# A two-block network in float32 on one core: start by feature tiles, GpSimd's products behind level 0, ScalarE's order in level 5

## What is computed

```python
def _mixer_gdn(h, w_in, conv_w, a_log, dt_bias, norm_g, w_out):
    proj = jnp.matmul(h, w_in)                      # 512x1024 @ 1024x4128
    qkv = silu(depthwise_conv(proj[..., :3072], conv_w))
    z, ba = proj[..., 3072:4096], proj[..., 4096:]  # ba: the gates
    ...                                             # q, k l2-normed per head
    beta = sigmoid(ba[:, :, 0])
    g = -exp(a_log) * softplus(ba[:, :, 1] + dt_bias)
    o = gated_delta(q, k, v, beta[0], g[0]) + flip(gated_delta(flip(q, k, v, beta[1], g[1])))
    o = rmsnorm(o, norm_g) * silu(z)                # per head
    return o @ w_out
```

## Time and profile before

| | |
|---|---|
| median of 3 runs | 2045.12 us |
| the profiled execution | 2043.4 us, span 2041.6 us |
| TensorE products | 1881.9 us busy (92%) |
| VectorE, ScalarE, GpSimd | 997.9, 726.0, 239.4 us busy |
| granted clock of TensorE, mean | 0.964 of 2.4 GHz |

### The profile page before, as it was taken

One profiled execution on the slowest core, in us unless ns is written; L12 is line 12 of the kernel. 1 busy time (PEld: TensorE's weight loads), 2 busy tenths in 40 slices (PEclk: granted clock), 3 DMA queues, 4 the chain that ended last, 5 costly groups with the idle time before them and its releaser, 6 DMA issues.

```text
span 2041.6 us, 24057 instructions
## 1 busy us (share of the span) xinstructions
PE 1881.9 (92%) x9070; PEld 1512.0 (74%) x9070; DVE 997.9 (49%) x1408; ACT 726.0 (36%) x1177; POOL 239.4 (12%) x226
## 2 busy tenths in 40 slices
PE   6999999999889999999799888889999998799989
PEld 6887778888668887887577677668887886575667
DVE  2775455555374444445321456464444366513653
ACT  2434544444222223322342343232223334434440
POOL 2001243343000001000000234000000000200410
PEclk8999999999989999999899999989999998899999
DMA  3223100000323324221222100423235231421001
GB/s 123 83 82 103 62 1 1 1 1 1 125 68 96 94 91 137 86 100 62 62 83 83 62 1 1 145 83 103 82 103 180 88 103 42 134 78 62 1 1 62
DMA packets 101442, 146.72 MB, mean 72 GB/s; under 512 B 4673, under 2 KB 70289, under 8 KB 101104
## 3 DMA queue, kind: packets, MB, share of 16 engines
q1 hardware_dynamic: 94272, 119.29, 18.6%
q0 software_dynamic: 6512, 24.20, 3.3%
q10 hardware_dynamic: 576, 2.10, 0.3%
HBM read 143.47 MB, written 2.10 MB: 71 GB/s over the span
## 4 chain that ended last, share of the span: by engine, by line
PE 86%; DVE 7%; ACT 3%; issue 2%; DMA 1%; POOL 1%; ACTq 0%; DVEq 0%; POOLq 0%; SPq 0%
PE bk L261 21%; PE bk L263 21%; PE bk L262 21%; PE bk L953 3%; PE bk L972 2%; PE bk L1711 1%; PE bk L2459 1%; PE bk L2460 1%; PE bk L963 1%; PE bk L2479 1%; ACT whi L246 1%; PE bk L940 1%; DVE wlo L252 1%; PE bk L1075 1%; PE bk L1014 1%
## 5 line engine op out<-in xcount | busy, mean ns | idle before, releaser
L252 DVE TENSOR_TENSOR wlo<-raw,whi 128x1024 fp32r<-128x1024 f32 x224 | 266.5, 1229 | 480.0 <-ACT whi L246 475.6
L261 PE MATMUL bk<-act_hi,whi 128*128 128x512 f32 (+1 forms) x1024 | 412.1, 402 | 7.6 <-DVE act_lo L387 5.0
L262 PE MATMUL bk<-act_lo,whi 128*128 128x512 f32 (+1 forms) x1024 | 409.2, 400 | 0.0
L263 PE MATMUL bk<-act_hi,wlo 128*128 128x512 f32 (+1 forms) x1024 | 409.0, 399 | 0.0
L246 ACT ACTIVATE whi<-raw 128x1024 fp32r<-128x1024 f32 x224 | 226.3, 1052 | 366.0 <-PE bk L263 327.7
L261 PE MATMUL bk<-whi,act_hi 128*128 128x512 f32 x768 | 310.7, 405 | 32.0 <-DVE act_lo L536 17.9
L263 PE MATMUL bk<-whi,act_lo 128*128 128x512 f32 x768 | 310.6, 404 | 0.0
L262 PE MATMUL bk<-wlo,act_hi 128*128 128x512 f32 x768 | 309.0, 402 | 0.0
L261 PEld LDWEIGHTS bk<-act_hi,whi 128*128 128x128 f32 (+1 forms) x1024 | 194.6, 190 | 60.2 <-issue 6.7
L262 PEld LDWEIGHTS bk<-act_lo,whi 128*128 128x128 f32 (+1 forms) x1024 | 194.7, 190 | 48.1 <-issue 0.7
L263 PEld LDWEIGHTS bk<-act_hi,wlo 128*128 128x128 f32 (+1 forms) x1024 | 194.5, 190 | 48.1
(11 more groups left out here) (372 smaller groups left out, 2381.0 us busy)
## 6 DMA issues: line engine op xcount, KB each, us to landing
raw<-in_mlp_w SPq DMA_DIRECT2D x128, 512.0 KB, 4.3
raw<-in_a_w_in SPq DMA_DIRECT2D x32, 512.0 KB, 4.5
work<-in_w_mod POOLq DMA_DIRECT2D x3, 4096.0 KB, 15.9
raw<-in_b_w_in SPq DMA_DIRECT2D x24, 512.0 KB, 3.9
raw<-in_w_in SPq DMA_DIRECT2D x14, 512.0 KB, 4.7
raw<-in_a_w_out SPq DMA_DIRECT2D x8, 512.0 KB, 4.0
raw<-in_b_w_out SPq DMA_DIRECT2D x8, 512.0 KB, 4.0
raw<-in_w_out SPq DMA_DIRECT2D x8, 512.0 KB, 3.9
```

Of the source, the lines that this page charges most:

```text
L252: nc.vector.tensor_tensor(wlo[b][:, hs], raw[hf][:, :], whi[b][:, hs], ALU.subtract).then_inc(w_ready, 1)
L261: nc.tensor.matmul(acc, lhs_hi, rhs_hi, start=first, stop=False, skip_group_check=True)
L262: nc.tensor.matmul(acc, lhs_hi, rhs_lo, start=False, stop=False, skip_group_check=True)
L263: return nc.tensor.matmul(acc, lhs_lo, rhs_hi, start=False, stop=last, skip_group_check=True)
```

## The change

- The identity is loaded first on SyncE's queue, then the left half of x's columns, half of slab 0, the right half, the other half of the slab. ScalarE's queue loads nothing any more. `tri`, `negpair`, parity and the gates' two vectors are issued by GpSimd at the end, after a wait for the right half of x. The convolution weights have a semaphore of their own.
- x is turned by feature tiles: one tile (4 transposes) fills one bank. The first output tile of slab 0 (bank 0) is multiplied feature tile by feature tile as these become ready, and tiles 4 to 7 are turned between the products. The second output tile (bank 1) follows, and then the gates. Slab 0 is split by halves among the split of the tiles on ScalarE and VectorE.
- GpSimd waits for `z` at 14h + 2 (level 0 done) before the logs and before the next head's decays; mask and start of Z stay ahead.
- ScalarE in level 5: the Ln of the head before comes ahead of the copies to X, in the place of the row exponential; the row exponential and then the Exp follow the copies.

```diff
+        def x_half(i):
+            return a["x"][0][:, i * 512:i * 512 + 512].rearrange("(t p) n -> p t n", p=P)
+
         def sp_start(sp):
-            for b in range(2):
-                load_slab(sp, 0, b, slab_source("a_in", 0, b))
-
-        def act_start(act):
-            for st in range(ST):
-                act.dma_start(X[:, st, :], a["x"][0, st * P:st * P + P, :]).then_inc(x_loaded, 16)
-
-        NCONST = 5
+            source = slab_source("a_in", 0, 0)
+            sp.dma_start(eye[:, :], a["k_eye"]).then_inc(eye_loaded, 16)
+            for i, loaded in enumerate((x_loaded, x_rest_loaded)):
+                sp.dma_start(X[:, :, i * 512:i * 512 + 512], x_half(i)).then_inc(loaded, 16)
+                sp.dma_start(slab_view(raw[i], KT // 2), source[:, i * KT // 2:(i + 1) * KT // 2, :]).then_inc(raw_loaded[i], 16)
+            load_slab(sp, 0, 1, slab_source("a_in", 0, 1))
+
+        NCONST = 4
         def pool_start(pool):
-            pool.dma_start(eye[:, :], a["k_eye"]).then_inc(eye_loaded, 16)
...
-            pool.dma_start(A["tri"], a["k_tri"].rearrange("p (m s) -> p m s", m=4)).then_inc(const_loaded, 16)
-            pool.dma_start(A["negpair"], a["k_negpair"].rearrange("p (m s) -> p m s", m=LEVELS)).then_inc(const_loaded, 16)
-            pool.dma_start(A["parity"], a["k_parity"]).then_inc(const_loaded, 16)
-            pool.dma_start(gwv["dt"], a["a_dt_bias"][0].rearrange("d h -> (d h)").partition_broadcast(P)
-                           ).then_inc(G["w_loaded"], 16)
-            pool.dma_start(gwv["alog"], a["a_alog"][0].rearrange("d h -> (d h)").partition_broadcast(P)
-                           ).then_inc(G["w_loaded"], 16)
...
+            pool.wait_ge(x_rest_loaded, 16)
+            pool.dma_start(A["tri"], a["k_tri"].rearrange("p (m s) -> p m s", m=4)).then_inc(const_loaded, 16)
+            pool.dma_start(A["negpair"], a["k_negpair"].rearrange("p (m s) -> p m s", m=LEVELS)).then_inc(const_loaded, 16)
+            pool.dma_start(A["parity"], a["k_parity"]).then_inc(const_loaded, 16)
...
+        def pe_start_turn(pe, kt):
+
+            if kt % 4 == 0:
+                pe.wait_ge((x_loaded, x_rest_loaded)[kt // 4], 16)
+            for st in range(ST):
+                mm = nc.tensor.transpose(bk[4 + kt % 4][:, st * P:st * P + P], X[:, st, kt * P:kt * P + P], eye[:, :])
+            mm.then_inc(xt_ready, 1)
+
         def pe_start(pe):
+            hi, lo = slab_view(whi[0], KT), slab_view(wlo[0], KT)
             pe.wait_ge(eye_loaded, 16)
-            for st in range(ST):
-                pe.wait_ge(x_loaded, 16 * (st + 1) if st == 3 else 64)
-                for hf in range(2):
-                    if st >= 2:
-                        pe.wait_ge(act_ready, 2 * (st - 2) + hf + 1)
-                    for k in range(4):
-                        kt = 4 * hf + k
-                        mm = nc.tensor.transpose(bk[2 * (st % 2) + hf][:, k * P:k * P + P],
-                                                 X[:, st, kt * P:kt * P + P], eye[:, :])
-                    mm.then_inc(xt_ready, 1)
-            pe.wait_ge(const_loaded, 16 * NCONST)
+            for kt in range(4):
+                pe_start_turn(pe, kt)
+            for kt in range(KT):
+                if kt % 4 == 0:
+                    pe.wait_ge(w_ready, kt // 4 + 1)
+                pe.wait_ge(act_ready, kt + 1)
+                mm = mm3(bk[0][:, :], hi[:, kt, 0:P], lo[:, kt, 0:P], act_hi[:, kt, :], act_lo[:, kt, :], kt == 0, kt == KT - 1)
+                if kt < 4:
+                    pe_start_turn(pe, kt + 4)
+            mm.then_inc(acc_ready, 1)
+            pe.wait_ge(conv_loaded, 16)
             nc.tensor.transpose(bk[4][:, 0:CONV * 24], vrow["conv"][0:CONV * 24, :], eye[0:CONV * 24, 0:CONV * 24]
                                 ).then_inc(vec_turned, 1)
+            for kt in range(KT):
+                mm = mm3(bk[1][:, :], hi[:, kt, P:2 * P], lo[:, kt, P:2 * P], act_hi[:, kt, :], act_lo[:, kt, :],
+                         kt == 0, kt == KT - 1)
+            mm.then_inc(slab_used, 1)
             pe.wait_ge(vec_loaded, 16 * NV_DMA)
             nc.tensor.transpose(bk[5][:, 0:NVEC], vrow["vec"][0:NVEC, :], eye[0:NVEC, 0:NVEC]).then_inc(vec_turned, 1)
 
+        def act_start_turned(act, kt):
+            act.wait_ge(xt_ready, kt + 1)
+            nc.scalar.activation(act_hi[:, kt, :], bk[4 + kt % 4][:, :], ACT.Copy).then_inc(act_hi_ready, 1)
+
+        def dve_start_turned(dve, kt):
+            dve.wait_ge(act_hi_ready, kt + 1)
+            nc.vector.tensor_tensor(act_lo[:, kt, :], bk[4 + kt % 4][:, :], act_hi[:, kt, :], ALU.subtract).then_inc(act_ready, 1)
+
+        def split_hi_half(act, hf):
+            act.wait_ge(raw_loaded[hf], 16)
+            hs = slice(hf * SLAB // 2, (hf + 1) * SLAB // 2)
+            nc.scalar.activation(whi[0][:, hs], raw[hf][:, :], ACT.Copy).then_inc(w_hi_ready, 1)
+
+        def split_lo_half(dve, hf):
+            dve.wait_ge(w_hi_ready, hf + 1)
+            hs = slice(hf * SLAB // 2, (hf + 1) * SLAB // 2)
+            nc.vector.tensor_tensor(wlo[0][:, hs], raw[hf][:, :], whi[0][:, hs], ALU.subtract).then_inc(w_ready, 1)
+
         def dve_start(dve):
-            split_lo(dve, 0, 0)
-            for st in range(ST):
-                dve_turned(dve, 0, st)
+            dve_start_turned(dve, 0)
+            split_lo_half(dve, 0)
+            for kt in range(1, 5):
+                dve_start_turned(dve, kt)
+            split_lo_half(dve, 1)
+            for kt in range(5, KT):
+                dve_start_turned(dve, kt)
             split_lo(dve, 0, 1)
+            dve.wait_ge(vec_turned, 1)
+            nc.vector.tensor_copy(convw[:, :], bk[4][:, 0:CONV * 24]).then_inc(vec_ready, 1)
             dve.wait_ge(G["w_hi"], 1)
             nc.vector.tensor_tensor(gw_lo, gw_raw, gw_hi, ALU.subtract).then_inc(G["w_ready"], 1)
-            dve.wait_ge(vec_turned, 1)
-            nc.vector.tensor_copy(convw[:, :], bk[4][:, 0:CONV * 24]).then_inc(vec_ready, 1)
             dve.wait_ge(vec_turned, 2)
             nc.vector.tensor_copy(cols[:, :], bk[5][:, 0:NVEC]).then_inc(vec_ready, 1)
             dve.wait_ge(vec_ready, 2)
...
         def pe_a_in(pe):
-            pe.wait_ge(act_ready, 8)
-            for b in range(2):
-                pe_feature_slab(pe, "a_in", 0, b)
-                if b == 0:
-                    pe_a_gates(pe)
+            pe_a_gates(pe)
+            pe_feature_slab(pe, "a_in", 0, 1)
             with pe.Fori(1, 7) as k2:
                 for b in range(2):
                     pe_feature_slab(pe, "a_in", k2, b)
@@ -1134,10 +1176,12 @@
             act.wait_ge(G["o_done"], h + 1)
             nc.scalar.activation(act_f[:, h, :], bk[3][:, :], ACT.Square).then_inc(G["o_sq"], 1)
 
-        def act_a_out_norm(act, h):
+        def act_a_out_log(act, h):
             act.wait_ge(G["qkn"], min(2 * h + 4, 2 * AH))
             act.wait_ge(G["o_sum"], h + 1)
             nc.scalar.activation(A["rs"][:, 1, :], bk[7][:, :], ACT.Ln, bias=RMS_EPS, scale=1.0 / P).then_inc(G["o_ln"], 1)
+
+        def act_a_out_exp(act, h):
             act.wait_ge(G["o_ln"], h + 1)
             nc.scalar.activation(A["rs"][:, 1, :], A["rs"][:, 1, :], ACT.Exp, scale=-0.5).then_inc(G["o_rs"], 1)
 
@@ -1152,8 +1196,8 @@
                     nc.scalar.activation(dst, src, ACT.Copy).then_inc(G["left"], 1)
                 if l == 4 and h > 0:
                     act_a_out_square(act, h - 1)
-                if l == 5:
-                    act_a_row_exp(act, h, 0)
+                if l == 5 and h > 0:
+                    act_a_out_log(act, h - 1)
                 if l == 6:
                     act_a_row_exp(act, h, 1)
                 for s in range(2):
@@ -1165,8 +1209,10 @@
                 if l == 4 and more:
                     act_a_rsqrt_log(act, h + 1, 0)
                     act_a_rsqrt_exp(act, h + 1, 0)
-                if l == 5 and h > 0:
-                    act_a_out_norm(act, h - 1)
+                if l == 5:
+                    act_a_row_exp(act, h, 0)
+                    if h > 0:
+                        act_a_out_exp(act, h - 1)
                 if l == 6:
                     if more:
                         act_a_rsqrt_log(act, h + 1, 1)
@@ -1180,7 +1226,8 @@
 
         def act_a_last(act):
             act_a_out_square(act, AH - 1)
-            act_a_out_norm(act, AH - 1)
+            act_a_out_log(act, AH - 1)
+            act_a_out_exp(act, AH - 1)
 
         def dve_a_key(dve, h):
             dve.wait_ge(G["l2_rs"], 2 * h + 1)
@@ -1343,6 +1390,8 @@
             if h > 0:
                 pool_a_scales(pool, h)
                 pool_a_unit(pool, h)
+            pool.wait_ge(G["z"], 14 * h + 2)
+            if h > 0:
                 pool_a_logs(pool, h)
             if h + 1 < AH:
                 pool_a_decays(pool, h + 1)
@@ -2687,7 +2736,6 @@
 
         @block.scalar
         def _(act):
-            act_start(act)
             act_begin(act)
             act_a_gates(act)
```

(28 more changed lines are left out.)

## The result

The changed kernel takes 2018.68 us (median of 4 runs, 2014.28 to 2020.43) against 2044.5 us beside it: a ratio of 0.987, 95% interval 0.9853 to 0.9887, so 25.8 us less, 23 to 30 by the interval. The forecast was 22.0 us less. The sign and the three places were right and the sum was too small: 2018.68 us lies just inside the range of 2018 to 2032 and just outside the 2019 to 2028.3 that the forecast had with its own bounds. The profiled execution took 2020.43 us, the slowest of the four, with a span of 2018.6 us. From here on lines have the numbers of each kernel's own text; in the changed kernel 953 is 995, 963 is 1005, 940 is 982, 972 is 1014, 1026 is 1068, 1140 is 1182, 1257 is 1304, 887 is 929 and 252 is 254.

A forecast was written before the change was run, and what follows sets the result against it. TensorE, busy 92% of the span, was taken to bound the kernel. Start 8.6, GpSimd's wait 5.2, ScalarE's order 7.1 and clock 1.1 sum to 22.0 us, so 2045.1 becomes 2023.1 us; range 2018 to 2032.

The forecast's parts named there:

- three places: Where TensorE's idle time or low clock could be won back: the start, the clock, the heads of mixer A.
- its own bounds: Whole kernel: the forecast without rivals, 2019 to 2028.3 us, given 73%.
- The start: Program start to gates: gates begin at 26.7 us instead of 35.36, gain 8.6 us, bounds 4 to 10.
- GpSimd's wait: Level 0 of the heads: 0.82 us for each of heads 1 to 6 plus 0.29 in head 0, 5.2 us.
- no harm from the moved products: GpSimd's products moved to levels 1 to 3 beside VectorE instructions reading PSUM: slowdown taken as zero.
- ScalarE's order: Level 5, Ln ahead of the copies: 1.01 us of idle time goes in heads 1 to 7, 7.1 us.
- rival 2: Level 5: ScalarE's gap too small, Ln delays copies and row sums, 3.5 us instead of 7.1, 2026.7; chance 8%.
- The clock in the heads: Two longer head periods: falls behind 1.58 us of idle time may go, 0 to 2.2 us, middle 1.1 taken.
- From there on the order is the old one: Behind the gates' begin: gates, second slab and loop follow as before, with the start's 8.6 us gain kept.
- The term of the clock: First slab: 1.4 us more, since the clock is at its lower level until about 13.5 us.
- Rival 1: Start: clock stays low through the first slab, gates begin as now, start gives nothing, 2031.7; chance 10%.
- a gap of 0.6 us: Start: TensorE's expected gap, to which the skill's rule that idle time between bursts halves the clock was applied.

The follow-up runs named there:

- heads only: GpSimd's wait and ScalarE's level-5 order together, start as before, against the kernel before: 2025.71 us, ratio 0.9919.
- start only: Only the start of the change, GpSimd and ScalarE in the heads as before, against the kernel before: 2035.18 us, ratio 0.9959.
- warm start: Changed kernel plus 20 unused TensorE products on a tile of ones before the wait for the identity: 2016.58 us, ratio 0.9865 to the kernel before.

## Why the prediction was too small

Two steps failed. The heads were worth more than forecast (18.0 us against 13.4), since waits were priced by the idle time in brackets. The start was worth less in the profile of the change (6.5 us against 8.6), since its gain was taken through the gates unchanged. That the sum missed by only 3.8 us is in part luck: the two errors point opposite ways.

**GpSimd's wait: right in mechanism, 5.2 us forecast, 7.2 measured.** The add at 0.62 us, 1.04 us of idle time left, no harm from the moved products: each as told. The step that failed is the price of a wait. I took the idle time in brackets. In the earlier trace rows the second product group of level 1 starts at 303.67 with 0.28 us of idle time. The timelines of before, in head 2 and then in head 7:

```profile
303.00 0.38 PE L963 MATMUL bk<-eye,work 128*128 128x128 f32 x2
303.67 0.75 PE L953 MATMUL bk<-work 128*128 128x128 f32 x4 [0.28 <-DVE work L1257]
304.26 0.38 PE L963 MATMUL bk<-eye,work 128*128 128x128 f32 x2
```

```profile
489.85 0.38 PE L963 MATMUL bk<-eye,work 128*128 128x128 f32 x2
490.06 0.65 PE L953 MATMUL bk<-work 128*128 128x128 f32 x4
490.55 0.38 PE L963 MATMUL bk<-eye,work 128*128 128x128 f32 x2
```

From start to start it is 0.67 + 0.59 us with the wait and 0.21 + 0.49 without: 0.56 us for a bracket of 0.28. Rows of dense products overlap by 0.17 us (the pair of transposes is 0.38 us long and the next row starts 0.21 us after it), and the bracket counts from the end; and the first group behind a wait takes 0.1 us longer. Both are lost at each wait. Counted so, GpSimd's wait gives 1.10 us a head (37.03 less 35.93), and 0.82 was the sum's term. With head 0's 0.6 us, where 0.29 stood in the sum, that is 7.2.

**ScalarE's order: 7.1 us forecast, 8.6 measured where it counts.** The same step: the bracket says 1.01, the periods 1.23 (35.93 less 34.70). Ln's 0.1 us of room was enough, the copy follows at once, rival 2 didn't come. 8.6 is 7 x 1.23; heads only and the change, which have this order and no fall, both have the period of 34.7 us.

**The clock in the heads: 1.1 forecast, 2.2 in the two profiles.** The middle between all and nothing was a hedge. Both falls went, and heads 1 to 7 have none in any of the nine other profiles in which the idle time of level 0 is 1.04 us or less. How many there are before varies, two in that profile and three in start only's. What I had not seen is that this term isn't one of its own: it belongs to GpSimd's part, and ScalarE's part alone would have made it worse by four falls. Why a shorter period meets a fall in every head and the longer one in two is open.

**The start: 8.6 us forecast, 7.9 at the gates' begin in the profile of the change, 6.5 behind them.** The step that failed is "From there on the order is the old one": the order is, but the gates' own length isn't. They took 1.4 us more here, and by the medians over the profiles 7.7 us at their begin are 6.2 at their end. The whole kernels give 7.6 us (25.8 less the 18.2 of the heads alone) and, start only, 8.4 to 9.5. Ahead of the gates the size was right, though not each term. In the profile of the change transfers and splits came 0.4 to 0.7 us later than worked out (the 0.5 us each for issue and landing stood on no row), and the clock rose at about 15.7 us, not 13.5; in four others x was there at 6.65 to 6.96, the clock up by about 12 us or before, and the gates began about a microsecond ahead of the forecast. The term of the clock was the wrong one to fix: it is 0 or about 1.7 us from one execution to the next. The masks and the gates' weights were in time: VectorE's gate subtract ran at 23.77. Rival 1 didn't come: the gaps ahead of the first product, up to 1.01 us (1.70 us in the warm start), didn't keep the clock down, and the first slab ran at the upper level. The Trainium skill (TensorE: Matmul & The Clock Gate, "HAM oscillation — how this bites in real kernels") tells of bursts parted by waits of about 3 to 5 us for transfers. The prediction took that over to a gap of 0.6 us, and it did not hold here. In the heads the trace agrees that idle time brings the clock down, but at shorter waits than the section's: falls behind 1.58 us, and not behind each, none behind 1.04.

The heads' terms sum to 6 x 1.10 + 0.6 + 7 x 1.23 + 2.2 = 18.0 us, where I had 13.4; the heads-only run measured 18.2. With 6.5 for the start that is 24.5, and line 1026 of the scan's end starts 24.3 us earlier; less the 1.3 us lost behind it, these are the 23.0 between the two spans. The medians differ by 25.8: the profile of the change was the slowest of its four executions. What the others had more isn't located.

## What to carry to other kernels

Price a wait on TensorE from start to start, against the same two groups where they run dense, and not by the idle time in brackets: here each short wait cost 0.2 to 0.3 us more than its bracket. Before a gain is added up, ask what a changed stage does to the clock: ScalarE's order alone brought six falls in place of two, and 8.6 us became 4. Follow a gain through the stage behind it too: of 7.7 us ahead of the gates 6.2 were left behind them. A gap that can't be closed can be filled with work that is ready, and a product with few columns is dear twice: one of 32 columns took 0.11 us here at the upper level, where one of 512 took 0.23, and the clock fell under them.

## What the runs showed of the hardware

- TensorE's lower level follows narrow products even when the engine is busy throughout: 96 products of 128x32 brought it from 2.4 to 1.2 GHz in all eleven profiles that have them, 2.1 to 5.8 us after their begin; 24 of 32x512 for the same numbers did not. At 0.11 us each the 96 would take 10.7 us, so it cost about 8 us of the gates' 18.6 in the changed kernel's profile, and it lasted 4 us into the next slab. Which property of the products does it, the columns or the weight load for each, isn't separated.
- In the profile's rows the granted clock reads 1.00 before the first recorded change, while durations show the lower level: 16 transposes in 3.65 us cold and in 1.91 us behind 6 us of other products (start of the program, changed kernel and warm start).
- A VectorE addition of two SBUF operands next to a GpSimd product took up to 1.43 us instead of 0.62, and a multiplication, seen once, 1.18 instead of 0.68; ones with a PSUM operand weren't touched (0.42 us).
